# First layer norm folded into shift and scale columns, and the matrix engine taking the first two chunks of a stage together

## The reference

```python
y_s = y_s * sigmoid(y_s @ w_glu + b_glu)
merged = sigmoid(ga) * (att @ w_att_br) + sigmoid(gb) * (y_s @ w_ssm_br)
x = LN(DN_ALPHA * x + (1 + g1) * (merged @ w_out), ln1_g, ln1_b)
h2 = x * (1 + sc2) + sh2
up = h2 @ w_up                      # 2048 -> 2 x 5632
conv = conv_b + sum_i conv_w[i] * ext[:, i:i+t]      # 3 taps along the tokens
val, gate = split(conv)
f = (gelu(gate) * val) @ w_down     # 5632 -> 2048
x = LN(DN_ALPHA * x + (1 + g2) * f, ln2_g, ln2_b)
```

## Time and profile before

| | us |
|---|---|
| median of three runs | 2376.44 (2372.89 to 2376.91) |
| the profiled execution, its own time | 2373.0 |
| its span, first to last instruction | 2371.2 |
| PE busy | 2183.9 (92%) |
| DVE busy | 1203.3 (51%) |
| ACT busy | 739.4 (31%) |
| POOL busy | 340.0 (14%) |

### The profile page before, as it was taken

The page is one execution under the profiler, slowest core; times in us unless marked ns, Lnnn a source line. Parts: engine busy times, 40 slices in busy tenths (PEclk is TensorE's granted clock), DMA queues, the critical chain, the costliest instruction groups (busy, mean ns, idle before and its releaser), DMA issues.

```text
span 2371.2 us, 41471 instructions
## 1 busy us (share of the span) xinstructions
PE 2183.9 (92%) x15407; PEld 1976.8 (83%) x15407; DVE 1203.3 (51%) x1786; ACT 739.4 (31%) x945; POOL 340.0 (14%) x632
## 2 busy tenths in 40 slices
PE   4869999999999888869999799999999999999996
PEld 2358788889999755539999689999999999999995
DVE  4743233323374344446654566644665456546665
ACT  1012222222222334433322354323333233233323
POOL 0104535300023301100000111000110001001002
PEclk8689999999899989979999979999999999999999
DMA  9899999996555897735676325446554655465441
GB/s 265 320 296 319 307 318 309 324 340 175 165 151 166 285 350 295 294 106 155 195 209 162 91 72 156 133 140 173 144 150 125 168 147 141 117 181 144 124 122 58
DMA packets 579059, 467.83 MB, mean 197 GB/s; under 512 B 17010, under 2 KB 503378, under 8 KB 578370
## 3 DMA queue, kind: packets, MB, share of 16 engines
q1 hardware_dynamic: 568971, 439.30, 61.1%
q0 software_dynamic: 6720, 19.64, 2.4%
q10 hardware_dynamic: 3264, 7.44, 0.9%
HBM read 440.13 MB, written 26.21 MB: 197 GB/s over the span
## 4 chain that ended last, share of the span: by engine, by line
PE 57%; DVE 4%; issue 2%; ACT 1%; DMA 1%; SPq 1%; POOL 1%; POOLq 0%; DVEq 0%; ACTq 0%
PE bank L947 16%; PE bank L949 16%; PE bank L948 16%; PE bank L1061 2%; PE bank L1126 1%; PE bank L1076 1%; PE bank L1206 1%; PE bank L1202 1%; DMA kpage<-in_cache_k 1%; POOL xT L816 1%; PE bank L1107 0%; PE bank L1110 0%; DVE hL L1999 0%; DVE res L1994 0%; ACT wH L1251 0%
## 5 line engine op out<-in xcount | busy, mean ns | idle before, releaser
L947 PE MATMUL bank<-hH,wH 128*128 128x320 f32 x2432 | 767.3, 316 | 25.1 <-DVE hL L1999 17.3
L948 PE MATMUL bank<-hL,wH 128*128 128x320 f32 x2432 | 758.1, 312 | 0.0
L949 PE MATMUL bank<-hH,wL 128*128 128x320 f32 x2432 | 757.8, 312 | 0.0
L1523 DVE TENSOR_TENSOR wL<-ring,wH 128x2048 fp32r<-128x2048 f32 (+3 forms) x208 | 391.3, 1881 | 268.3 <-ACT wH L1251 268.3
L947 PEld LDWEIGHTS bank<-hH,wH 128*128 128x128 f32 x2432 | 462.3, 190 | 67.7 <-issue 48.1
L948 PEld LDWEIGHTS bank<-hL,wH 128*128 128x128 f32 x2432 | 463.0, 190 | 0.0
L949 PEld LDWEIGHTS bank<-hH,wL 128*128 128x128 f32 x2432 | 462.6, 190 | 0.0
L1251 ACT ACTIVATE wH<-ring 128x2048 fp32r<-128x2048 f32 (+3 forms) x208 | 330.1, 1587 | 381.6 <-PE bank L949 376.2
L1528 DVE TENSOR_TENSOR wL<-pring,wH 128x2048 fp32r<-128x2048 f32 x64 | 177.1, 2769 | 369.3 <-ACT wH L1256 368.7
L947 PE MATMUL bank<-fH,wH 128*128 128x320 f32 x704 | 218.7, 311 | 11.2 <-DVE fL L2032 11.2
L948 PE MATMUL bank<-fL,wH 128*128 128x320 f32 x704 | 218.2, 310 | 0.0
(11 more groups left out here) (383 smaller groups left out, 2872.6 us busy)
## 6 DMA issues: line engine op xcount, KB each, us to landing
ring<-in_w_ada SPq DMA_DIRECT2D x96, 1024.0 KB, 11.0
ring<-in_w_up SPq DMA_DIRECT2D x88, 1024.0 KB, 5.8
pring<-in_w_in SPq DMA_DIRECT2D x64, 1024.0 KB, 8.2
kpage<-in_cache_k SPq DMA_DIRECT2D x64, 512.0 KB, 5.9
vpage<-in_cache_v SPq DMA_DIRECT2D x64, 512.0 KB, 5.7
ring<-in_w_down SPq DMA_DIRECT2D x32, 768.0 KB, 5.0
ring<-in_w_down SPq DMA_DIRECT2D x32, 640.0 KB, 4.5
ring<-in_w_out SPq DMA_DIRECT2D x16, 1024.0 KB, 6.0
```

The source lines that it names most:

```text
L947: t.matmul(acc, a[:, k, :], high[:, k, :], start=(k == 0), stop=False)
L948: t.matmul(acc, a[:, k, :], low[:, k, :], start=False, stop=False)
L949: last = t.matmul(acc, b[:, k, :], high[:, k, :], start=False, stop=(k == K - 1))
L1523: v.tensor_tensor(wL[cc % 2][:, 0:K, :], ring[cc][:, 0:K, :], wH[cc % 2][:, 0:K, :].bitcast(F32), SUB)\
```

## The change

In the first layer norm, gain and bias no longer go through ACT per tile. DVE once multiplies the `h2` scale columns by the gain, adds bias times scale to the shift columns, and multiplies gain and bias by alpha for the later residual. `xT` then holds the normalised value without gain and bias; `down3`'s residual applies them (one more DVE instruction per chunk, of 64 columns). DVE instead of POOL multiplies by `rstd`; ACT instead of DVE makes the prompt part of `h2`; DVE keeps the samples.

On PE, the first two chunks of `out`, `up0` and the four down stages are taken together (`first_pair`): it waits for the weights of both, then in `up0` alternates the two chunks tile by tile, and in the others does all but the last two tiles of the first chunk, all but the last two of the second, and then the last two tiles of both in turn. The first chunk of `merge` no longer waits for `s`. The written-out pass is now the first one instead of the last.

```diff
@@ gpsimd
-            layer_norm(0)
@@ tensor
-            pe.wait_ge(S["s_ready"], KA)
-            operands = [(attH, attL), (sH, sL)]
-            passes(pe, "merge", None, 0, lambda i, _: [products(i, MERGE, cc, KA, *operands[cc % 2]) for cc in range(4)])
-            passes(pe, "out", None, 0, lambda i, _: [products(i, OUT, cc, KD, mH, mL, (S["m_ready"], 1) if cc == 0 else None) for cc in range(4)])
+            def first_pair(n0, K, high, low, ready, alternate=False):
+
+                for cc in range(2):
+                    pe.wait_ge(S["split_done"], n0 + cc + 1 + RING)
+                    pe.wait_ge(acc_free[cc], nth_pair(n0) + 1)
+
+                def step(cc, k):
+                    acc = bank[cc][:, 0:T]
+                    t.matmul(acc, wH[cc][:, k, :], high[:, k, :], start=(k == 0), stop=False)
+                    t.matmul(acc, wH[cc][:, k, :], low[:, k, :], start=False, stop=False)
+                    return t.matmul(acc, wL[cc][:, k, :], high[:, k, :], start=False, stop=(k == K - 1))
+
+                held = 0 if alternate else K - 2
+                for cc in range(2):
+                    for k in range(held):
+                        if cc == 0:
+                            pe.wait_ge(ready[0], ready[1] + k + 1)
+                        step(cc, k)
+                last = [None, None]
+                for k in range(held, K):
+                    pe.wait_ge(ready[0], ready[1] + k + 1)
+                    for cc in range(2):
+                        last[cc] = step(cc, k)
+                        if k == K - 1:
+                            last[cc].then_inc(S["chunk_done"], 1)
+
+            def stage(name, K, high, low, ready=None, alternate=False):
+                n0 = first_of[name]
+                if ready:
+                    first_pair(n0, K, high, low, ready, alternate)
+                    for cc in (2, 3):
+                        products(0, n0, cc, K, high, low)
+                with pe.Fori(1 if ready else 0, passes_of[name]) as i:
+                    for cc in range(4):
+                        products(i, n0, cc, K, high, low)
+
+            def merge_pass(i, first=False):
+                for cc in range(4):
+                    if first and cc == 1:
+                        pe.wait_ge(S["s_ready"], KA)
+                    products(i, MERGE, cc, KA, *((sH, sL) if cc % 2 else (attH, attL)))
+
+            merge_pass(0, first=True)
+            with pe.Fori(1, passes_of["merge"]) as i:
+                merge_pass(i)
+            stage("out", KD, mH, mL, (S["m_ready"], 1))
...
+                stage(f"up{q}", KD, hH, hL, (S["h2_ready"], 0) if q == 0 else None, alternate=True)
+                stage(f"down{q}", nj, fH, fL, (S["f_ready"], down + 1))
@@ scalar
-            for k in range(KD + 1):
-                if k < KD:
-                    gain(k, 0, 96, 112, S["gained"])
-                if k >= 1:
-                    act.wait_ge(S["modulated"], k)
-                    a.activation(hH[:, k - 1, :], res[(k - 1) % 2][:], ACT.Copy).then_inc(S["h2_hi"], 1)
+            SH2, SC2 = 3 * KD, 4 * KD
+            for k in range(KD):
+                if True:
+                    act.wait_ge(S["scaled"], k + 1)
+                    if k >= 2:
+                        act.wait_ge(S["h2_ready"], k - 1)
+                    own.mark(a.activation(res[k % 2][:, 0:NP], xT[:, k, 0:NP], ACT.Identity, scale=mod[:, SC2 + k, 0:1], bias=mod[:, SH2 + k, 0:1]))
+                    own.settle()
+                    act.wait_ge(S["modulated"], k + 1)
+                    a.activation(hH[:, k, :], res[k % 2][:], ACT.Copy).then_inc(S["h2_hi"], 1)
@@ vector
-            def residual(src, m, gain, ready, free=None, r=res[0]):
+            def residual(src, m, gain, ready, free=None, r=res[0], normed=False):
...
+                if normed:
+                    own.step(v.tensor_scalar(r[:, NP:T], r[:, NP:T], shift, None, ADD))
...
+            dve.wait_ge(S["x_pre"], KD + 1)
+            own.step(v.tensor_tensor(shifted, mod[:, SC2:SC2 + KD, :], columns(112), MUL))
+            own.mark(v.tensor_tensor(mod[:, SH2:SH2 + KD, :], mod[:, SH2:SH2 + KD, :], shifted, ADD))
+            own.step(v.tensor_tensor(mod[:, SC2:SC2 + KD, :], mod[:, SC2:SC2 + KD, :], columns(96), MUL))
+            own.step(v.tensor_scalar(par[:, 96:128], par[:, 96:128], ALPHA, None, MUL))
             layer_norm(0)
+            dve.wait_ge(S["rstd_ready"], 1)
 
             for k in range(KD + 1):
                 if k < KD:
-                    dve.wait_ge(S["gained"], k + 1)
+                    v.tensor_tensor(xT[:, k, :], xT[:, k, :], rstd[:], MUL).then_inc(S["scaled"], 1)
+                    dve.wait_ge(S["scaled"], k + 1)
                     tmp = res[k % 2]
-                    own.mark(v.tensor_scalar(tmp[:, 0:NP], xT[:, k, 0:NP], mod[:, SC2 + k, 0:1], mod[:, SH2 + k, 0:1], MUL, ADD))
                     own.step(v.tensor_tensor(samples(tmp), samples(xT[:, k, :]), per_sample(mod[:, SC2 + k, 1:NC]), MUL))
                     v.tensor_tensor(samples(tmp), samples(tmp), per_sample(mod[:, SH2 + k, 1:NC]), ADD).then_inc(S["modulated"], 1)
```

More of the change, by code:

```diff
@@ L268, in hybrid_step @@
                  "s_ready m_ready x_pre mean_done centred squared var_done var_ready "
-                 "sd_ready rstd_ready scaled gained modulated h2_hi normed h2_ready conv_landed halo conv_ev gelu_done f_ready ext_read "
+                 "sd_ready rstd_ready scaled modulated h2_hi normed h2_ready conv_landed halo conv_ev gelu_done f_ready ext_read "
                  "rows_stored y_out angle_ready c_ready bias_spread").split():
@@ L1944, in _ @@
             passes(dve, "merge", own, 4, merge_pass)
-            def residual(src, m, gain, ready, free=None, r=res[0]):
+            def residual(src, m, gain, ready, free=None, r=res[0], normed=False):
                 col = mod[:, ds(m + gain, 1), :].rearrange("p o c -> p (o c)")
-                own.mark(v.tensor_scalar(r[:, 0:NP], src[:, 0:NP], col[:, 0:1], None, MUL))
+                scale, shift = (par[:, ds(m + 96, 1)], par[:, ds(m + 112, 1)]) if normed else (ALPHA, None)
+                own.mark(v.tensor_scalar(r[:, 0:NP], src[:, 0:NP], col[:, 0:1], shift, MUL, ADD) if normed else
+                         v.tensor_scalar(r[:, 0:NP], src[:, 0:NP], col[:, 0:1], None, MUL))
                 ins = v.tensor_tensor(samples(r[:]), samples(src), per_sample(col[:, 1:NC]), MUL)
@@ L1956, in residual @@
                     own.step(ins)
+                if normed:
+                    own.step(v.tensor_scalar(r[:, NP:T], r[:, NP:T], shift, None, ADD))
                 x = xT[:, ds(m, 1), :].rearrange("p o t -> p (o t)")
-                v.scalar_tensor_tensor(out=x, in0=x, scalar=ALPHA, in1=r[:], op0=MUL, op1=ADD).then_inc(ready, 1)
+                v.scalar_tensor_tensor(out=x, in0=x, scalar=scale, in1=r[:], op0=MUL, op1=ADD).then_inc(ready, 1)
             dve.wait_ge(S["x_landed"], 48)
@@ L1987, in _, with columns @@
             read_turns(conv_state_turns())
+            def columns(first):
+                return par[:, first:first + KD].unsqueeze(2).to_broadcast([P, KD, NC])
+            shifted = res[0][:, 0:KD * NC].rearrange("p (k c) -> p k c", c=NC)
+            dve.wait_ge(S["x_pre"], KD + 1)
[3 more added lines that the diff above has]
+            own.step(v.tensor_scalar(par[:, 96:128], par[:, 96:128], ALPHA, None, MUL))
             layer_norm(0)
+            dve.wait_ge(S["rstd_ready"], 1)
             for k in range(KD + 1):
                 if k < KD:
-                    dve.wait_ge(S["gained"], k + 1)
+                    v.tensor_tensor(xT[:, k, :], xT[:, k, :], rstd[:], MUL).then_inc(S["scaled"], 1)
+                    dve.wait_ge(S["scaled"], k + 1)
                     tmp = res[k % 2]
-                    own.mark(v.tensor_scalar(tmp[:, 0:NP], xT[:, k, 0:NP], mod[:, SC2 + k, 0:1], mod[:, SH2 + k, 0:1], MUL, ADD))
                     own.step(v.tensor_tensor(samples(tmp), samples(xT[:, k, :]), per_sample(mod[:, SC2 + k, 1:NC]), MUL))
@@ L2049, in down_pass @@
                             dve.wait_ge(acc_free[cc % 2], i * 2 + (nth_pair(n0) + cc // 2 + 2))
-                            residual(y, i * 4 + cc, G2, S["x_pre"], r=res[1])
+                            residual(y, i * 4 + cc, G2, S["x_pre"], r=res[1], normed=True)
                             dve.wait_ge(S["x_pre"], i * 4 + (KD + cc + 2))
-                passes(dve, f"down{q}", own, 8 if q == len(QUARTERS) - 1 else 0, down_pass)
+                passes(dve, f"down{q}", own, 12 if q == len(QUARTERS) - 1 else 0, down_pass)
                 j0 += nj
```

## The result

The changed kernel took 2404.38 us (median of 4 runs, 2401.34 to 2410.13); the kernel before took 2376.45 beside it. The ratio is 1.0123, 95% interval 1.0108 to 1.0137: slower, by 25.7 to 32.6 us. The forecast was 2394 and slower. The sign and the new waits held, the term for the clock did not: the loss is 28 us where 18 were forecast, 0.4 us above the top of the range (2380 to 2404) and 4.4 above the forecast's own (2388 to 2400). The profiled execution took 2402.69 (span 2401.1). One execution of a later experiment (*`merge` waits as before*) took 7304.79 us, and the ratio leaves it out.

What follows compares the result with a forecast made beforehand. PE, busy 92% of the span, was taken as the bound, so only its waits and lower clock count. Terms -4.3 + 7.3 + 12.5 - 7.6 + 0.3 = +8.2, plus 9.6 for the clock, +17.8: 2394 us, range 2380 to 2404.

Steps and rivals of the forecast that it cites:

- `merge`, -4.3: Start of `merge`: the 2.90 us wait for `s` and 1.8 us of slow matmuls go, -4.3 us.
- `out`, +7.3: Start of `out`: PE stands 4.3 us ahead of the pair and 4.1 behind it, with no old wait to gain: +7.3 us.
- the down stages, +12.5: Starts of `down0` to `down3`: old 2.8 us wait replaced by two of 5.7 to 6.9 together per stage, +12.5 us.
- the weights come in time: Rival for all pairs: the third chunk's weights are ready before the pair ends, no new wait arises; 2345, chance 0.05.
- `up0`, -9.2: `up0`: earlier `h2` tiles bring the third chunk to 1384.95 instead of 1394.2, despite 5.6 us of standing: -9.2 us.
- its restart, +1.6: `up0`, third chunk: after the standing PE restarts at the lower clock for some 12 matmuls, +1.6 us.
- everything runs cold: Rival: all ten new waits lower the clock (+24.2), PE stays slow through `up0`'s pair (3.1): +27, 2404, chance 0.13.
- The clock, 9.6: `out` and down stages: six of ten new waits lower the clock, at 1.6 us each: +9.6 us.
- upper bound: Whole kernel: all ten new waits in `out` and the down stages lower the clock, sum +24.2 us.
- the clock holds: Rival: no new wait in `out` or down stages lowers the clock: +8.2, or +6.6 with warm `up0` restart; 2384, chance 0.18.
- Gains and waits cancel: Rival: the clock holds and `h2` tiles come at the old 1.25 us, 3 us sooner: +4 to +5, 2381, chance 0.06.

Runs made afterwards that it cites:

- `merge` waits as before: The kernel without held pairs, with the first chunk of `merge` waiting for all of `s` again: 2374.07 us, ratio 0.9986.
- kernel without held pairs: The changed kernel, with the first two chunks of `out` and the down stages one after the other as before: 2366.98 us, ratio 0.9963.
- late-wait run: The changed kernel, with pairs in `out` and down stages awaiting the second chunk's weights only ahead of that chunk's first matmul: 2375.08 us, ratio 0.9997.
- run with the tile put between: The kernel without held pairs, with chunk 0's last tile taken after six tiles of chunk 1 in the down stages: 2356.06 us, ratio 0.9908.
- run with filled waits: The changed kernel, with PE's standing times in `out`, `up0` and the down stages filled with matmuls nobody reads: 2384.04 us, ratio 1.0039.

## Why the prediction was right about the waits and wrong about the clock

**`merge`, -4.3: right.** No wait for `s`; the second chunk is done by 1106.19, where the forecast was near 1105.2 from a start 0.9 us earlier, and the 3.5 us between the two copies are 24 matmuls at the full clock. From `glu` to the layer norm the kernel without held pairs is 4.1 us shorter than before.

**`out`, +7.3, and the down stages, +12.5: right to within 0.7 us a stage.** Forecast 4.3 and 4.1 in `out`; 4.54 and 3.89 came. Forecast 3.8 and 3.1 at 12 tiles; 3.98 and 2.92. Forecast 3.3 and 2.4 at 10 tiles; 3.49 and 2.45. The rival *the weights come in time* fell at the point it named: ACT takes the third chunk's copy only when the pair is all but done. The late-wait run shows that the front half hangs on one line of waits, the run with the tile put between that the back half hangs on ending both chunks at once.

**`up0`, -9.2: right; its restart, +1.6: measured 2.4.** PE's first matmul comes 16.55 us after the second sum starts at 1349.80 (forecast 16.5), the third chunk 27.82 us after that (forecast 28.0), with a wait of 5.63 (5.6). The clock rose within the pair, as I took it to: the granted clock is 0.50 for its first 5.6 us and 1.00 for the rest. So *everything runs cold*, whose 2404 comes nearest to the time, held in its half on the falls (all but one) and was wrong in its half on `up0` (its 3.1 us there should read 1382.6 - 1379.2 = 3.4). ACT's unseen instruction took 0.60, inside its bounds of 0.38 and 0.65, and delays only the last tile. The restart had 19 matmuls at the low clock, not some 12.

**The clock, 9.6: the step that failed.** I wrote: "I count the four longest and two of the other six: 6 x 1.6 = 9.6". Nine of ten lowered it, at 1.9 us each by the windows: 17.0. Both factors were low. The four longest all fell, as counted; of the other six five fell, not two. Of the 7.4 us that were missing, the three falls more are 4.8 at the price I had, and the price, 0.3 too low nine times, is 2.6. The count came from five old waits in a single execution, of which two did harm; I carried that share to the six waits of 2.4 to 3.5 us as if it were known. From `merge` to the end of `down3`, over all the profiles of this study and leaving out the later waits for `h2` tiles, where the clock was low already, waits of 2.4 to 3.0 us lowered the clock in 23 of 30 cases, those of 3.4 to 5.7 us in 12 of 13, and those up to 1.7 us never. The upper bound that I had stated, all ten, was the better forecast: +24.2. The Trainium skill (TensorE: Matmul & The Clock Gate, section "HAM oscillation — how this bites in real kernels") tells of a kernel whose pieces of matmul work are shorter than the waits between them, and every piece there starts at the low clock. No run here has work of that shape: a held pair alone is 8.8 to 14.1 us of work by my sum, more than twice the wait ahead of it, so it was wrong of me to read from that section that all ten fall. That nine of ten fell is the trace's own finding, and why one of the two waits of 3.49 us lowered the clock and the other did not stays open.

The account from `glu` on: +29.0 measured, +17.8 forecast. Of the 11.2 between them, 7.4 are the falls (17.0 - 9.6), 0.8 the restart in `up0` (2.4 - 1.6). 3.0 are left. The run with filled waits has nearly the same remainder without any fall: +9.3, where my sum without any clock term is +6.6. It has no one place: with the span cut at the second sum, at the first matmuls of `up1`, `up2` and `up3` and at the first sum of the second layer norm, 0.3 to 0.7 us are left in each stretch, in both profiles alike. Some of it shows: the waits ahead of the held pairs are 0.2 us longer than forecast in five places (those behind are 0.2 shorter in three), and PE waits 1.09 instead of 0.67 us ahead of the second layer norm. The cause of the rest, about 2 us, stays open.

The rival *the clock holds* (2384) was built as a kernel by filling the waits: it came 10.3 us above the kernel before on its chip, where this rival had +8.2, or +6.6 with a warm restart in `up0`. *Gains and waits cancel* fails on the 1.45 us between tiles and on the nine falls.

## What to carry to other kernels

Where chunks pass through two weight buffers, the chunk that runs is the cover under which the next chunk's weights are made; two chunks that end together leave that work bare behind the pair, and awaiting both chunks' weights at once leaves it bare ahead of the pair as well. To hide a late last tile, take it in the middle of the second chunk, so that the first buffer comes free while work is left (here, with `out` in plain order and the rest of the change, 2356 us against 2375 before). And price a new wait on a busy TensorE at more than its length: in this kernel 35 of 43 waits of 2.4 to 5.7 us lowered the clock, at 1.9 us each in the changed kernel.

## What the runs showed that I had not expected

A wait can be made harmless to the clock by matmuls that nobody reads: 240 of them took 20 us off the changed kernel. How often a wait of the same length lowers the clock differs between executions (two of four and four of four at the same `fL` waits of 2.6 to 3.0 us), which moves a run by some 3 us. And the same code ahead of `glu` ended up to 7.6 us apart in these profiles (1063.8 to 1071.5), so that a difference under 5 us is better read from a stretch of the trace than from the whole span.
